# Values computed with tokens stationary, and 128-column products in place of padded 256-column ones

## The reference

```python
z = u @ w_in[l]                       # u: 512 x 1024
(a_q, a_k, a_v, b_q, b_k, b_v, b_f, c_q, c_k, c_v, g) = jnp.split(z, split_idx, axis=-1)
# a: differential attention, 4 heads of 2 x 64 (one value of 128 columns for both softmaxes)
# b: forgetting attention, 8 heads of 64; c: stick-breaking attention, 8 heads of 64
# all causal, in blocks of 128 queries
logits = jnp.einsum('bqhd,bkhd->bhqk', qb, k) * scale + bias
p = jax.nn.softmax(jnp.where(dist >= 0, logits, -jnp.inf), axis=-1)   # a: p0 - lam * p1
out = jnp.einsum('bhqk,bkhe->bhqe', p, v)
```

## Time and profile before

| | |
|---|---|
| median of 3 runs | 2437.34 us |
| the profiled execution | 2437.91 us |
| its span, first to last instruction | 2436.1 us |
| busy in the span: TensorE, VectorE, ScalarE | 100%, 87%, 61% |
| granted TensorE clock | 1.00 |
| one tile of the mixer (the third, 483.4 to 554.9 us) | 71.5 us; VectorE busy 65.23, ScalarE 57.39 |

### The profile page before, as it was taken

The page is one execution under the profiler, slowest core; times in us unless marked ns, Lnnn a source line. Parts: engine busy times, 40 slices in busy tenths (PEclk is TensorE's granted clock), DMA queues, the critical chain, the costliest instruction groups (busy, mean ns, idle before and its releaser), DMA issues.

```text
span 2436.1 us, 48109 instructions
## 1 busy us (share of the span) xinstructions
PE 2426.0 (100%) x15514; PEld 2211.0 (91%) x15514; DVE 2129.7 (87%) x3960; ACT 1493.0 (61%) x2917; POOL 4.0 (0%) x14
## 2 busy tenths in 40 slices
PE   9999999999999999999999999999999999999999
PEld 8999888888899889998889998888888998899988
DVE  8999878999898779998699997789998986899985
ACT  6666457887754456664366664578786554566643
POOL 0000000000000000000000000000000000000000
PEclk9999999999999999999999999999999999999999
DMA  4333322212232323333333323321212333233332
GB/s 162 113 104 104 113 96 69 74 58 78 62 113 78 113 87 104 105 106 118 102 102 108 103 95 105 103 79 61 72 60 70 105 105 104 87 106 105 117 113 78
DMA packets 64676, 233.72 MB, mean 96 GB/s; under 512 B 7168, under 2 KB 7552, under 8 KB 64512
## 3 DMA queue, kind: packets, MB, share of 16 engines
q1 hardware_dynamic: 64368, 231.58, 29.1%
q10 hardware_dynamic: 144, 0.10, 0.0%
HBM read 229.55 MB, written 2.10 MB: 95 GB/s over the span
## 4 chain that ended last, share of the span: by engine, by line
PE 96%; DVE 2%; ACT 1%; DMA 1%; issue 0%; SPq 0%; DVEq 0%; ACTq 0%
PE ps L715 30%; PE ps L717 30%; PE ps L716 30%; PE ps L988 2%; PE ps L1031 1%; PE ps L978 1%; PE ps L979 1%; PE ps L1030 1%; DMA w_raw<-weights 1%; DVE w_lo L1997 0%; PE ps L994 0%; PE ps L1042 0%; PE ps L1043 0%; ACT w_hi L1293 0%; PE ps L962 0%
## 5 line engine op out<-in xcount | busy, mean ns | idle before, releaser
L1293 ACT ACTIVATE w_hi<-w_raw 128x512 fp32r<-128x512 f32 (+1 forms) x874 | 622.3, 721 | 475.4 <-PE ps L717 226.6
L1997 DVE TENSOR_TENSOR w_lo<-w_raw,w_hi 128x512 fp32r<-128x512 f32 (+1 forms) x874 | 699.1, 805 | 105.5 <-ACT w_hi L1293 88.9
L715 PE MATMUL ps<-u_hi,w_hi 128*128 128x256 f32 (+1 forms) x2432 | 786.0, 323 | 0.9 <-DVE w_lo L1997 0.9
L717 PE MATMUL ps<-u_hi,w_lo 128*128 128x256 f32 (+1 forms) x2432 | 781.1, 321 | 0.0
L716 PE MATMUL ps<-u_lo,w_hi 128*128 128x256 f32 (+1 forms) x2432 | 780.2, 321 | 0.0
L716 PE MATMUL ps<-area,w_hi 128*128 128x256 f32 (+1 forms) x1778 | 583.4, 328 | 0.0
L715 PEld LDWEIGHTS ps<-u_hi,w_hi 128*128 128x128 f32 x2432 | 463.3, 190 | 37.4 <-issue 2.4
L717 PEld LDWEIGHTS ps<-u_hi,w_lo 128*128 128x128 f32 x2432 | 463.2, 190 | 35.1
L716 PEld LDWEIGHTS ps<-u_lo,w_hi 128*128 128x128 f32 x2432 | 463.4, 191 | 32.9
L715 PE MATMUL ps<-area,w_hi 128*128 128x512 f32 (+1 forms) x1414 | 482.0, 341 | 1.0 <-ACT scratch_whole L1392 0.9
L717 PE MATMUL ps<-area,w_lo 128*128 128x512 f32 (+1 forms) x1414 | 480.1, 340 | 0.0
(11 more groups left out here) (220 smaller groups left out, 2909.9 us busy)
## 6 DMA issues: line engine op xcount, KB each, us to landing
w_raw<-weights SPq DMA_DIRECT2D x432, 512.0 KB, 3.7
h<-x SPq DMA_DIRECT2D x4, 512.0 KB, 6.8
out<-scratch_whole SPq DMA_DIRECT2D x8, 256.0 KB, 2.0
scratch_whole<-const_b SPq DMA_DIRECT2D x1, 512.0 KB, 10.1
scratch_whole<-const_r SPq DMA_DIRECT2D x1, 192.0 KB, 9.2
cst<-const SPq DMA_DIRECT2D x1, 137.0 KB, 8.6
par<-params ACTq DMA_DIRECT2D x1, 98.0 KB, 4.9
```

What stands on the lines that cost most here:

```text
L715: pe.matmul(dst, hi, x_hi, start=start, stop=False, **kw)
L717: return pe.matmul(dst, lo, x_hi, start=False, stop=stop, **kw)
L1293: return act.activation(dst, src, ACT.Copy)
L1997: return dve.tensor_tensor(dst, src, hi_part.bitcast(F32), ALU.subtract)
```

## The change

It has these parts.

- The three values of a tile are computed together with the tokens as the stationary operand: for token block j and feature block k three products of 384 columns (128 for each of a, b and c) in place of 512-column products with stationary weights. The results have tokens on partitions at once. `turn_values` and the three value `take`s go; the factor of the RMS norm is applied per token by `values_hi` and `values_lo`, and for that `turn_rstd` transposes `rstd` once a layer. The weights of the three values are laid out so that the 24 blocks fill three units; at k == 2 the three blocks lie at the end of slot 2 and the start of slot 0, and the product is split into 256 and 128 columns.
- `value_steps(begin, end)` issues 32 steps (j = 0, 1 for all k, then j = 2, 3), cut into pieces between the head's work. A tile uses units c, c, values (3), b, b, a, a.
- Scores of query block 0 and weighted products of key block 3 are 128 columns wide, the zeros are gone, and `score_products` and `weighted_products` place them between wider ones.
- Work is reordered on all three engines; a unit's bank and slot follow the new order; the values get a place of their own in `area`.

```diff
-PT_OFF = K_OFF[:-1] + [K_OFF[-1] + P]
-PT_SIZE = TRI + P
-WIDE = 2 * P
+PT_OFF, PT_SIZE = K_OFF, TRI
...
+            def score_products(queries, keys_of):
+
+                for i, part in ((0, 0), (1, 0), (0, 1), (1, 1), (2, 0), (2, 1), (3, 0), (3, 1)):
+                    n = (i + 1) * P
+                    last = pe.matmul(ps[:, SB0 + i, 0:n], queries[part][:, i * P:n], keys_of[part][:, 0:n],
+                                     start=part == 0, stop=part == 1)
...
+            def value_steps(begin, end, before):
...
+                    columns = ((0, 2), (2, 3)) if k == 2 else ((0, 3),)
+                    for x, w, part in ((x_hi, w_hi, 0), (x_lo, w_hi, 1), (x_hi, w_lo, 2)):
+                        for first, after in columns:
+                            b = (2 * UNIT + 3 * k + first) % (SLOTS * UNIT)
+                            last = pe.matmul(ps[:, val_banks(before)[j], first * P:after * P], x, w[:, b * P:(b + after - first) * P],
...
+            def weighted_products(parts):
+
+                n_parts = len(parts(0))
+                steps = [(j, part) for j in range(2) for part in range(n_parts)]
+                steps += [(j, part) for part in range(n_parts) for j in (2, 3)]
...
             def rest_of_tile(unit):
 
                 unit(0)
                 turn_probs(1)
-                turn_values(0)
                 unit(1, 0, 3)
                 weighted(1, 1)
                 scores(0, 0)
...
-                unit(8, 0, 2)
-                turn_probs(0)
-                turn_values(1)
-                unit(8, 2)
-                weighted(1, 0)
+                unit(own[3], 2, 0, 4)
+                turn_probs(0)
+                unit(own[3], 2, 4)
+                weighted(t, 1, 0)
                 scores(1, 1)
```

On VectorE, in `heads`, around the first head of b (rows of the weights left out):

```diff
                 turned_lo(0)
                 turned_lo(1)
                 turned_lo(2)
                 turned_lo(3)
-                values_lo(1)
-                take(7, 1.0)
-                qk_lo(0, 0, 6)
-                take(8, 1.0)
+                take(0, banks[2], SCALE)
+                take(1, banks[3], 1.0)
                 block_max(1, 0)
                 block_max(1, 1)
                 block_max(1, 2)
-                qk_lo(0, 2, 7)
+                qk_lo(0, 0, 0)
                 block_max(1, 3)
+                qk_lo(0, 2, 1)
                 output_lo(2, t)
                 share_out(1, 0, prob_set)
```

```diff
-                next_unit(1, 1.0)
+                next_unit(1, 1, 1.0)
+                split(1)
                 output_lo(1, t - 1)
                 differences(layer)
-                split(1)
```

More of the change, by code:

```diff
@@ L973, in scores @@
                     pe.wait_ge(max_set, c.next(max_set, NQ))
[L975 to L980, removed]
+                score_products((q_twice(branch, hd), q_rest(branch, hd)), (k_both(branch, hd), k_bias(branch, hd)))
             def turn_probs(buf):
@@ L989, in turn_probs, with turn_rstd @@
                 last.then_inc(probs_turned, 1)
-            def turn_values(st):
+            def turn_rstd():
                 for j in range(NQ):
[L994 to L1001, removed]
@@ new lines, in weighted_products @@
+            def weighted_products(parts):
+                n_parts = len(parts(0))
+                steps = [(j, part) for j in range(2) for part in range(n_parts)]
+                steps += [(j, part) for part in range(n_parts) for j in (2, 3)]
+                for j, part in steps:
+                    if part == 0:
+                        pe.wait_ge(pt_set, c.next(pt_set))
+                    n = (NQ - j) * P
+                    v, at = parts(j)[part]
+                    last = pe.matmul(ps[:, OB, SEQ - n:SEQ], v, area[:, at + PT_OFF[j]:at + PT_OFF[j] + n],
+                                     start=(j, part) == (0, 0), stop=(j, part) == steps[-1])
+                last.then_inc(o_mm, 1)
@@ L1024, in weighted @@
                     pe.wait_ge(o_norm, c.next(o_norm))
[L1026 to L1032, removed]
+                weighted_products(lambda j: ((val_block(t, branch, hd, j), PT_HI), (val_block(t, branch, hd, j), PT_LO)))
             def stick_scores(hd):
@@ L1037, in stick_scores @@
                     pe.wait_ge(qk_set, c.next(qk_set, 2))
[L1038 to L1043, removed]
+                score_products((q_twice(2, hd), q_rest(2, hd)), (k_both(2, hd), k_both(2, hd)))
             def diff_norm(bank=AUX):
@@ L1048, in diff_norm, with unit @@
                 pe.matmul(ps[:, bank, :], ones_r[:], o_sq_lo, start=False, stop=True).then_inc(o_ms, 1)
[L1050 to L1055, removed]
+            def unit(bank, k, first_block=0, end=UNIT, first=False):
+                last = u_unit(bank, k, (first_block, end), first)
@@ L1109, in heads @@
-                weighted(2, 1)
-                scores(1, 0)
-                unit(7, 4)
-                unit(8, 0, 2)
-                turn_probs(0)
-                turn_values(1)
-                unit(8, 2)
-                weighted(1, 0)
+                else:
+                    pe.wait_ge(v_set, c.next(v_set, 2))
+                own = (AUX, 0, 1, AUX) if before else (0, AUX, 1, AUX)
+                unit(own[0], 2, 0, 5)
+                weighted(t, 2, 0, before)
+                stick_scores(1)
@@ L1122, in mixer @@
             def mixer():
[L1123 to L1130, removed]
-                    if end == UNIT:
-                        last.then_inc(unit_done, 1)
-                rest_of_tile(gate)
-                pe.wait_ge(v_set, c.peek(v_set))
-                gate(2, 0, 7)
+                heads(0, False)
+                for t in range(1, NT):
+                    heads(t, True)
+                rest_of_tile(NT - 1, unit)
+                bank_read()
+                unit(2, 2, 0, 7)
                 turn_probs(0)
-                gate(2, 7)
+                unit(2, 2, 7)
                 pe.wait_ge(o_set, c.peek(o_set, 3 * NT - 2))
@@ L1719, in heads @@
                 stick_sigmoids(3)
+                if not before:
+                    values_hi(t, 0, before)
+                    values_hi(t, 1, before)
                 split(2)
@@ L2620, in output_lo @@
             def output_lo(branch, t):
-                at = (t + branch * NT) * SEQ
+                rounded, rest = (area[:, o_at(branch, t, part):o_at(branch, t + 1, part)] for part in range(2))
                 src = o_whole[:]
@@ L2718, in heads @@
                 turned_lo(3)
-                take(6, SCALE)
+                split(2)
+                qk_lo(1, 2, 1)
                 split(0)
```

298 lines of the change are left out of this document (161 added, 137 removed).

## The result

| | before | after |
|---|---|---|
| median of the runs | 2437.19 us (17 runs) | 2441.96 us (17 runs) |
| ratio after to before | | 1.0019, 95% interval 1.0012 to 1.0026 |
| the profiled execution, and its span | 2437.91, 2436.1 us | 2442.05, 2439.9 us |
| period of a tile, from b's second `turn_probs(1)` to the next tile's | 71.48 us | 71.87 us |

A forecast was written before the change was run, and what follows sets the result against it. TensorE, busy 2426.0 of 2436.1 us, was taken as the bound. Its work (-1.6 us) and three waits (+6.4, +1.6, +1.3) sum to +7.7, taking the median from 2437.34 to 2445.0 us; range 2432 to 2453.

The forecast's parts named there:

- TensorE's own work: Work on TensorE per tile: values 0.19 us less, other narrowed products 0.12 less; 2.5 us less in eight tiles.
- second wait: First scores of b: TensorE waits 0 to 0.4 us for b's key, taken as 0.2; 1.6 us in all.
- The price of a narrow product: Cost of a 128-column fp32r product on TensorE, shown by no row: taken as 0.115 us, between 0.067 and 0.22.
- The first wait: Transposes of b's second head: TensorE waits 0.8 us a tile for the fourth row of probabilities; 6.4 us in all.
- E: Time at which the ten transposes of b's first head end on TensorE; later times are counted from it.
- The third: turn_probs(0) in each layer's last rest_of_tile: stop of 0.06 us becomes about 0.75; 1.3 us in two layers.
- The wait behind the wait: First copy for weighted_whole: charged nothing, but would take about as much if the first wait were gone.
- no waits: Rival: queues 0.8 us faster than counted, so only TensorE's work is left; 2435.7 us, chance 0.22.
- More waits than found: Rival: further waits in the first tile or at the weighted heads; 2452 us, chance 0.09.
- Cheap narrow products: Rival: 128-column products run at their streaming rate, 0.067 us; 2434 us, 2422 without waits; chance 0.10.
- plain-rate ones: Rival: 128-column products fall to the plain fp32 rate, 0.22 us; 29.4 us more, 2469 us; chance 0.11.
- The other side, not slower: Not slower if VectorE's fourth row of probabilities is ready by E + 11.4 instead of E + 12.1; same 0.34, faster 0.12.

The follow-up runs named there:

- the row of pairs: Kernel after, with back-to-back rows of fp32r products in five column-width combinations added ahead of turn_rstd's four transposes in each layer; 2462.94 us.

## Why the prediction was right, point by point

The mechanism was right: less work on TensorE, and waits for VectorE that take more than it gives. The outcome it held likeliest, slower, was just missed by its own measure: 2441.96 lies 0.2 us under the 2442.2 that it drew as the line, and it is the 17 runs of each kernel that set the 4.8 us apart from nothing.

- **TensorE's own work**, forecast -0.31 us a tile. With 0.93 to 1.03 us of waits in a tile (0.88, and 0.05 to 0.15) the period rose by 0.39, so the work fell by 0.54 to 0.64, about twice as much. From start to next start, a tile's units, values and value transposes went from 49.84 + 1.15 to 33.09 + 17.66, 0.24 less (forecast 0.19); scores and weighted products from 14.82 to 14.72, which without the second wait is 0.15 to 0.25 less (forecast 0.12, and 0.15 when done alone); the rest, 0.16, stands at the probabilities' transposes without their wait. I priced products in their steady rows and left out the seams between kinds of work; that the new order gains just there is the likely reading, which no run tests by itself. Over eight tiles this is 4.3 to 5.1 us in place of 2.5, and it is the term that was mis-sized.
- **The price of a narrow product**, taken as 0.115 between 0.067 and 0.22: 0.11. Products of 384 columns, forecast 0.173 to 0.175: fifteen of them in a row,

```profile
440.94 0.33 PE L1030 MATMUL ps<-w_hi,u_lo 128*128 128x384 f32 x1
...
443.37 0.33 PE L1030 MATMUL ps<-w_hi,u_hi 128*128 128x384 f32 x1
```

 start 2.43 us apart in 14 steps, 0.1736 each.
- **The first wait**, forecast 0.8 us from a chain to E + 12.1 against an arrival at E + 10.70: 0.88 from E + 12.16 against E + 10.74. The tile came to 71.87 us, not 72.2, by the term above. The links fall on the forecast too: `take` done at E + 3.11 (forecast 3.11), ScalarE's eight operations until E + 8.0 (8.0), the last exponential until E + 11.2 (11.3).
- **The second wait**, forecast 0.2, was 0.05 to 0.15 in most tiles and 0.47 in the first tile of each layer, which I had not worked out by itself: 1.2 to 1.8 us in all for 1.6. That the two agree is luck: less than forecast in six tiles, and more than twice in the other two.
- **The third**, forecast as a stop of 0.75 that adds 0.65 a layer: the stop was 0.51, so 0.36 a layer; undoing its cause gave 0.45. The prediction had 0.06 for the stop before, though its own row (1.40 for 1.25) shows 0.15.
- **`turn_rstd`**, 0.44 a layer as forecast.
- **VectorE's work**, which the sum didn't use: forecast 1.6 us less a tile, measured 0.5 (65.23 to 64.73). The eight operations on the values take 0.34 or 0.47 us each, 3.3 us a tile. ScalarE got 0.5 more for a forecast of 0.6.
- **The wait behind the wait**: "were that gone, this one would take about as much". It took 0.49 of 0.69 when TensorE's block was moved.

The sum of the terms as measured: TensorE's work -4.3 to -5.1 and `turn_rstd` +0.9, 7.0 of first, 1.2 to 1.8 of second and 0.7 of third waits make +5.3 to +5.6. The two mixers of the traces grew by 5.5; the medians differ by 4.8, and what is shorter outside the mixers is only in part explained.

The rivals: no waits is excluded by the transposes. More waits than found came only as the 0.47 us in the first tiles, far from 2452. Cheap narrow products and plain-rate ones are excluded by the row of pairs: 107 to 117 ns for 128 columns in any company. The Trainium skill, "TensorE: Matmul & The Clock Gate", section "Back-to-back issue gap", has about 81 ns for 128 columns in a sustained stream; that is not reached here. The same page of the Trainium skill, section "LDWEIGHTS (loading the stationary operand)", has 107 ns for the load of 128 columns; the measured prices agree with that as a lower bound. The other side, not slower, was to come out if VectorE were done by E + 11.4. The versions that take that wait away do come out at the level of before (2438.0 with only that one gone), and under it when the waits behind it go too.

## What to carry to other kernels

When one engine is busy all of the time, the gain of a change is read from start-to-start times of that engine, and its price from the chain on the others up to each point where that engine asks for a result; here the chain could be summed from the old trace to within 0.1 us. A wait that is removed uncovers the next one, so the moves must be tried together: alone, two of them gave 0.5 and -2.0 us, and with the others 8.8. A change that takes work off the busiest engine should not be given up at +0.2% before its order has been mended; most of this loss hung on one `take` that stood behind four copies.

## What the runs showed of the hardware

A 128-column fp32r product with its own stationary operand is paid at 0.107 to 0.117 us even beside a product of 512 columns, whose own turn of 0.227 us is twice that. So a long product builds up no lead for the short one after it: narrowing 256 columns to 128 saves 0.01 us, not half. The numbers are those of a load that hides only behind the product directly ahead (0.338 us expected for 512 and 128 columns, 0.344 measured), but no run separates the load from another fixed cost of a product.

A short stop of TensorE hardly shows as its idle time: 0.88 us of waits in ten transposes leave 0.22 us of idle in the tile, and the list of waits has them under the weight loads, not under the products. And a stop costs more than itself: 0.19 us ahead of the norm's products came with 0.11 at the first of them.
